# Two hybrid blocks on one core: repeated key heads projected once and copied inside SBUF, and the delta net's rates and products by beta placed elsewhere

## The reference, cut to what matters

```python
# first block, attention branches (of z = rms_norm(x) @ w_in)
q = partial_rope(q, cos, sin)                       # 4 heads of 64
k = partial_rope(k[:, :, None, :], cos, sin)[:, :, 0]     # ONE key head of 64 for the 4
iq = partial_rope(iq, icos, isin)                   # 8 index heads of 32
ik = partial_rope(ik[:, :, None, :], icos, isin)[:, :, 0] # ONE index key of 32 for the 8
sc = einsum('bqhs,bqh->bqs', relu(iq . ik * 32 ** -0.5), iw)   # the 128 largest are kept
out = softmax(q . k, kept) @ v * silu(g)
# second block
q = axial_rope(rmsnorm(aq, q_norm_w)); k = axial_rope(rmsnorm(ak, k_norm_w))
#   8 query heads, 2 key heads, 4 queries to a key
attn = softmax(q . k / 8) @ v
beta = sigmoid(b_raw); g = -exp(a_log) * softplus(a_raw + dt_bias)   # 2 directions x 8 heads
# delta net by chunks of 64 tokens, both directions:
L = where(strict, (k * beta) @ k.T * decay, 0); T = inverse(eye + L)
u = T @ (v * beta)
```

## Time and profile before

| | us |
|---|---|
| median of 3 runs | 2613.02 (2611.95 to 2616.01) |
| the profiled execution | 2617.88 |
| its span, first to last instruction | 2616.1 |
| TensorE busy | 2328.5 (89%) |
| VectorE busy | 989.2 (38%) |
| ScalarE busy | 453.4 (17%) |
| GpSimd busy | 218.0 (8%) |

### The profile page before, as it was taken

One profiled execution on the slowest core, in us unless ns is written; L12 is line 12 of the kernel. 1 busy time (PEld: TensorE's weight loads), 2 busy tenths in 40 slices (PEclk: granted clock), 3 DMA queues, 4 the chain that ended last, 5 costly groups with the idle time before them and its releaser, 6 DMA issues. The chain is left out here.

```text
span 2616.1 us, 44161 instructions
## 1 busy us (share of the span) xinstructions
PE 2328.5 (89%) x18735; PEld 1240.4 (47%) x18735; DVE 989.2 (38%) x1789; ACT 453.4 (17%) x851; POOL 218.0 (8%) x174
## 2 busy tenths in 40 slices
PE   7989989969898898987898977889979969999998
PEld 3543438624363343953444433589634444444442
DVE  1166785232026667523224442464321151111112
ACT  1011432010102143201122332222110020000000
POOL 0111300000010220000003630400000000000000
PEclk9999999989898999998988998899989979999999
DMA  4134010020214301002101101100013439999997
GB/s 151 57 146 160 9 45 3 23 81 32 101 45 180 131 4 44 4 22 89 65 25 57 49 25 53 45 3 5 34 65 121 198 139 401 421 422 422 422 422 301
DMA packets 60439, 328.25 MB, mean 125 GB/s; under 512 B 6880, under 2 KB 9440, under 8 KB 31200
## 3 DMA queue, kind: packets, MB, share of 16 engines
q1 hardware_dynamic: 60256, 325.63, 31.9%
HBM read 320.88 MB, written 4.72 MB: 124 GB/s over the span
## 5 line engine op out<-in xcount | busy, mean ns | idle before, releaser
L420 PE MATMUL ps<-store,side_ring 128*128 128x512 f32 x832 | 420.0, 630 | 20.5 <-DMA side_ring<-in_w_rwkv 8.1
L420 PEld LDWEIGHTS ps<-store,side_ring 128*128 128x128 f32 x832 | 146.6, 196 | 188.9 <-issue 165.3
L2346 PE MATMUL ps<-expert_ring,xe 128*64 128x512 f32 x1024 | 224.8, 597 | 2.7 <-DVE back L2455 1.7
L333 PE MATMUL ps<-store,side_ring 128*128 128x512 f32 x384 | 169.9, 606 | 1.9 <-DVE store L299 1.9
L2346 PEld LDWEIGHTS ps<-expert_ring,xe 128*64 128x64 f32 x1024 | 73.3, 138 | 150.8 <-issue 148.7
L333 PEld LDWEIGHTS ps<-store,side_ring 128*128 128x128 f32 x384 | 74.6, 195 | 96.1 <-issue 93.8
L2374 PE MATMUL ps<-expert_ring,store 128*64 128x512 f32 x512 | 113.2, 600 | 1.4 <-DVE store L2431 1.4
L1437 PE MATMUL ps<-store,weight_ring 128*128 128x512 f32 x256 | 112.0, 593 | 1.9 <-DVE store L299 1.9
L2116 PE MATMUL ps<-store,expert_ring 128*128 128x512 f32 x224 | 99.1, 606 | 11.6 <-DMA expert_ring<-in_w_merge 11.6
L420 PE MATMUL ps<-store 128*128 128x512 f32 x160 | 78.9, 647 | 12.6 <-DMA store<-in_w_merge 12.1
L2403 ACT ACTIVATE store<-ps 128x1024 f32<-128x1024 f32 x16 | 16.4, 1024 | 419.2 <-PE ps L2346 419.2
(11 more groups left out here) (420 smaller groups left out, 3885.8 us busy)
## 6 DMA issues: line engine op xcount, KB each, us to landing
expert_ring<-in_w_expert SPq DMA_DIRECT2D x192, 1024.0 KB, 16.2
mixed<-in_w_ada SPq DMA_DIRECT2D x24, 1024.0 KB, 5.0
side_ring<-in_w_attn SPq DMA_DIRECT2D x34, 512.0 KB, 3.6
side_ring<-in_w_rwkv SPq DMA_DIRECT2D x20, 512.0 KB, 4.4
weight_ring<-in_ple_gate SPq DMA_DIRECT2D x16, 512.0 KB, 3.4
side_ring<-in_w_conv SPq DMA_DIRECT2D x12, 512.0 KB, 3.3
store<-in_w_merge SPq DMA_DIRECT2D x10, 512.0 KB, 3.6
expert_ring<-in_w_merge SPq DMA_DIRECT2D x3, 1536.0 KB, 6.2
```

The lines of the kernel that those rows point to most:

```text
L333: last = nc.tensor.matmul(ps[:, u, :], ring[:, u, k, :], src[:, k, :], start=(k == 0), stop=(k == kt - 1))
L420: ins = self.nc.tensor.matmul(self.ps[:, self.banks[j % banks], :], self.ring[:, j % self.slots, k, :], self.src[:, k, :], start=(k == 0), ...
L2346: last = nc.tensor.matmul(ps[w, 2 * ep + half, :], xe[:, ep, k, :], ring[:, unit % SLOTS, k2, S * half:S * half + S], start=(k == 0), stop ...
```

## The change

In the first block A_K becomes one tile of the key head (rows 0 to 63) and the index key twice (rows 64 to 127); A_IK is a place in `z` that is no longer projected. The A_K tile is turned first, in two halves with their own tables, and SP copies the turned index key to four quarters of A_IK and the key head to rows 64 to 127 of A_K. The first gate tile moves into `project`, and its SiLU to the head of `index_topk`; the side work there has 9 tiles instead of 10. In the second block the two key heads share one tile (the query heads are put in pairs p and p + 4), so `normed_heads` has five tiles; the rates are 32 more columns of its values, copied by ScalarE, and the `by_head` tile is gone. They lie token-major, and four matmuls bring them into place. The product of `low` with beta moves to GpSimd in the spread stage, and `bv` to ScalarE in the chunk stage. The diff, cut to its core:

```diff
-A_Q, A_K, A_DQ, A_DK, A_IQ, A_IK, A_G, A_DG, N_A = 0, 2, 3, 6, 9, 11, 12, 14, 17
+A_Q, A_K, A_DQ, A_DK, A_IQ, A_G, A_IK, N_A = 0, 2, 3, 6, 9, 11, 13, 16
...
-    SEMAPHORES = dict(rotated=0, scaled=0, rot_used=0, added=0)
+    SEMAPHORES = dict(rotated=0, scaled=0, rot_used=0, added=0, ik_copied=0, k_copied=0)
+    KEYS = ((slice(0, HD), "head"), (slice(HD, P), "index"))
...
+    def parts(self, j):
+        table = self.jobs[j][1]
+        return self.KEYS if table == "keys" else ((slice(0, P), table),)
+
+    def parts_until(self, j):
+        return sum(len(self.parts(i)) for i in range(j))
+
...
     def rotate(self, pe, upto):
         for j in range(self.issued, upto):
-            tile, table = self.jobs[j]
+            tile = self.jobs[j][0]
             if j < 4:
-                pe.wait_ge(self.kept[0][j], self.kept[1])
+                bank = tile % 4
+                pe.wait_ge(self.kept[0][bank], self.kept[1])
             else:
-                pe.wait_ge(self.s["rot_used"], j - 3)
-            self.nc.tensor.matmul(self.M.ps[:, j % 4, :], self.M.c(f"rot_{table}"), self.z[:, tile, :], start=True,
-                                  stop=True).then_inc(self.s["rotated"], 1)
+                pe.wait_ge(self.s["rot_used"], self.parts_until(j - 3))
+            for rows, name in self.parts(j):
+                last = self.nc.tensor.matmul(self.M.ps[rows, j % 4, :], self.M.c(f"rot_{name}")[rows, rows], self.z[rows, tile, :],
+                                             start=True, stop=True)
+            last.then_inc(self.s["rotated"], 1)
...
+            for n, (rows, table) in enumerate(self.parts(j)):
+                if j or n:
+                    pool.wait_ge(self.s["scaled"], self.parts_until(j) + n)
+                self.nc.gpsimd.tensor_tensor(self.z[rows, tile, :], self.z[rows, tile, :], self.M.table(f"cos_{table}")[rows],
+                                             ALU.mult).then_inc(self.s["scaled"], 1)
...
+            for rows, table in self.parts(j):
+                self.nc.vector.tensor_tensor(self.turned[rows, j % 2, :], self.M.ps[rows, j % 4, :],
+                                             self.M.table(f"sin_{table}")[rows], ALU.mult).then_inc(self.s["rot_used"], 1)
+            dve.wait_ge(self.s["rot_used"], self.parts_until(j + 1))
+            dve.wait_ge(self.s["scaled"], self.parts_until(j + 1))
...
+    def repeat_keys(self, sp):
+
+        z = self.z
+        sp.wait_ge(self.s["added"], 1)
+        for q in range(4):
+            sp.dma_start(z[32 * q:32 * q + 32, A_IK, :], z[HD:HD + 32, A_K, :]).then_inc(self.s["ik_copied"], 16)
+        sp.wait_ge(self.s["ik_copied"], 64)
+        sp.dma_start(z[HD:P, A_K, :], z[0:HD, A_K, :]).then_inc(self.s["k_copied"], 16)
+        sp.wait_ge(self.s["k_copied"], 16)
...
+                if turn:
+                    turn.repeat_keys(sp)
...
+                nc.scalar.activation(raw_gate, raw_gate, ACT.Silu).then_inc(s["gate_ready"], 1)
...
+                act.wait_ge(s["gate_ready"], 1)
...
-            kept = project(nc, M, w_attn, A_G, KT, h, 4, keep, ready, ring)
-            turn = Turning(nc, M, z, [(t, "head") for t in range(A_IQ)] + [(t, "index") for t in range(A_IQ, A_IK + 1)], kept,
+            kept = project(nc, M, w_attn, A_G + 1, KT, h, 4, keep, ready, ring)
+            turn = Turning(nc, M, z, [(A_K, "keys"), (A_Q, "head"), (A_Q + 1, "head")] + [(t, "head") for t in range(A_DQ, A_IQ)]
+                           + [(t, "index") for t in range(A_IQ, A_IQ + 2)], kept,
...
-        side = SideProjection(nc, M, [silu(j) for j in range(A_G, N_A)] + [mixed(j) for j in range(early)], KT, h, ring,
+        side = SideProjection(nc, M, [silu(j) for j in range(A_G + 1, N_A)] + [mixed(j) for j in range(early)], KT, h, ring,
...
+        ring, w = sb("weight_ring", [P, 3, KT, P]), sb("token_weights", [P, KT, P + 32])
...
                 for i in range(n):
                     project(i)
-                    if 1 <= i <= 4:
+                    if i >= 1:
                         add_up(i - 1)
-                add_up(4)
-                spread(0, 0)
-                spread(1, 1)
                 pe.wait_ge(s["v_landed"], 16)
                 values(0)
-                add_up(5)
-                pe.wait_ge(s["kept"], 6)
-                spread(2, 2)
+                add_up(4)
+                values(1)
+                spread(0, 0)
+                pe.wait_ge(s["kept"], 5)
+                spread(1, 1)
                 pe.wait_ge(s["normed"], 1)
-                spread(3, 0)
-                values(1)
+                spread(2, 0)
+                spread(3, 2)
                 pe.wait_ge(s["normed"], 2)
                 rotate(0, 1)
                 pe.wait_ge(s["normed"], 3)
-                rotate(1, 2)
+                rotate(1, 0)
+                values(2)
                 pe.wait_ge(s["normed"], 4)
-                rotate(2, 0)
-                values(2)
+                rotate(2, 2)
                 pe.wait_ge(s["rot_used"], 1)
                 rotate(3, 1)
                 pe.wait_ge(s["rot_used"], 2)
-                spread(4, 2)
+                spread(4, 0)
+                values(3)
                 pe.wait_ge(s["rot_used"], 3)
-                spread(5, 0)
-                values(3)
-                pe.wait_ge(s["rot_used"], 4)
-                rotate(4, 1)
-                pe.wait_ge(s["normed"], 5)
-                rotate(5, 2)
+                rotate(4, 2)
...
+                    nc.scalar.activation(rates[:, t, :], ps[:, 4 + t, P:P + 32], ACT.Copy).then_inc(s["v_kept"], 1)
...
                     keep(i)
+                keep_values(0)
                 root(0)
-                keep(5)
-                keep_values(0)
+                keep_values(1)
                 root(1)
-                for t in range(1, TT):
+                for t in range(2, TT):
                     keep_values(t)
...
-            kv = pair // 2
-                jobs.append(Pair(q=z[:, pair, here], k=z[:, 4 + kv, :], keys=S, bias=None,
-                                 v=[(tok[:, t, HD * kv:HD * kv + HD],) * 2 for t in range(TT)],
+                jobs.append(Pair(q=z[:, pair, here], k=z[:, 4, :], keys=S, bias=None,
+                                 v=[(tok[:, t, 0:HD], tok[:, t, HD:P]) for t in range(TT)],
-        by_head = (a["w_ba2"], lambda act, made: nc.scalar.activation(rates, made, ACT.Copy))
-        side = SideProjection(nc, M, [mixed(j) for j in range(12)] + [by_head], KT, h, sb("side_ring", [P, 4, KT, P]), 4, (6, 7))
...
-                    for c in range(NCH):
-                        for w in halves:
-                            last = nc.tensor.matmul(ps[w, 0, 16 * c:16 * c + 16], rates[w, c * CH:(c + 1) * CH],
-                                                    M.c("ident2")[w, 0:16], start=True, stop=True)
+                    by_chunk = ps[:, 0, 0:16 * NCH].rearrange("p (t c x) -> p t c x", c=2, x=16)
+                    for hp, w in enumerate(halves):
+                        for c in range(2):
+                            last = nc.tensor.matmul(by_chunk[w, :, c, :], M.c("ident")[:, c * CH:(c + 1) * CH],
+                                                    rates[:, :, 16 * hp:16 * hp + 16], start=True, stop=True)
...
-                    pool.wait_ge(s["masked"], 2 * NCH)
+                        pool.wait_ge(s["masked"], 2 * n + 2)
+                        nc.gpsimd.tensor_tensor(low[:, n], low[:, n], beta[:, n].unsqueeze(3).broadcast_to([P, 2, JP, CH]),
+                                                ALU.mult).then_inc(s["by_beta"], 1)
+                    pool.wait_ge(s["by_beta"], NCH)
...
+                            pe.wait_ge(s["v_scaled"], 2 * JP * (c - 1))
...
+                @block.scalar
+                def _(act):
+                    for c in range(NCH):
+                        act.wait_ge(s["made"], c + 1)
+                        for d, n in ((0, c), (1, NCH - 1 - c)):
+                            for j in range(JP):
+                                nc.scalar.activation(bv[:, n, d, j, :], bank4(4 * (c % 2) + 3)[:, j, :], ACT.Identity,
+                                                     scale=beta[:, n, d, j:j + 1]).then_inc(s["v_scaled"], 1)
...
-                            own.mark(nc.vector.tensor_tensor(low[:, n, d], bank4(b), low[:, n, d], ALU.mult))
+                            own.mark(nc.vector.scalar_tensor_tensor(out=low[:, n, d], in0=bank4(b), scalar=-1.0, in1=low[:, n, d],
+                                                                    op0=ALU.mult, op1=ALU.mult))
                             own.mark(nc.vector.tensor_tensor(at[:, n, d], bank4(b + 1), at[:, n, d], ALU.mult))
                             own.mark(nc.vector.tensor_tensor(kd[:, n, d], bank4(b + 2), wide(decay_out), ALU.mult))
-                            own.step(nc.vector.tensor_tensor(bv[:, n, d], bank4(b + 3), wide(beta), ALU.mult))
```

(13 more changed lines are left out.)

55 lines of the change are left out of this document (22 added, 33 removed).

## The result

The changed kernel takes 2569.18 us (median of 4 runs, 2565.97 to 2569.99) against 2614.52 for the kernel before (2611.95 to 2617.49): a ratio of 0.9823, 95% interval 0.9808 to 0.9839. The forecast was 2570.2. The profiled execution has a span of 2567.9 us, 48.2 us under the one of before.

What follows compares the result with a forecast made beforehand. A chain of stages with barriers, each bound by its last engine: 14.9 + 8.0 + 7.6 + 13.3 - 0.2 - 0.8 = 42.8 us, from the median 2613.02 to 2570.2 us; range 2565 to 2582.

Steps and rivals of the forecast that it cites:

- Index stage and rotations: First block: TensorE ends the index stage, 6.8 us gained; halved rotations in the token stage save 0.6; 7.4 a layer.
- The two copies in series: Token stage: SP's key copies inside SBUF take some 5 us, hidden under 28 us of the same stage.
- Normed heads: Second block: five projected tiles for six, with two token products under the first inversion's wait; gain 8.0 us (6.5 to 8.5).
- Attention of the second block: Rate tile leaves the side work, 96 products for 104; the stage gains 7.6 us (4.6 to 8.8).
- about 1.5 us remain and 3 are gained: Second block's attention: of TensorE's 4.7 us of waits for ScalarE to free a bank, 3 us go (bounds 0 and 4.7).
- GpSimd is late next: End of the second block's attention: GpSimd ends last at 1543.8, VectorE at 1542.4 with one more 0.8 us step.
- Rival B: Second block's attention tail: bank waits stay, or GpSimd's last nine operations stretch; 3 to 4 us lost, 2574; chance 0.13.
- Chunk stage: Delta net's chunk products: TensorE replaces VectorE as bound, 2.42 us a chunk for 4.06; gain 13.3 us (9 to 14).
- Rival A: Chunk stage stays with ScalarE (2.75 us a chunk) or a half clock; 2.5 to 3.5 us come back, 2573; chance 0.17.
- Rates and spread: Rates stage: fewer matmuls gain nothing, side products wait for a load. Spread stage: beta on GpSimd costs 0 to 0.5, taken 0.2.
- Semaphores: Ends of stages: clearing costs 0.1 us per semaphore; eight more clearings lose 0.8 us.
- a sign of being wrong by over 5 us: Stages not touched: if one shifts its clock, the forecast is wrong by more than 5 us.

Runs made afterwards that it cites:

- e4: Changed kernel with a tenth side tile in the index stage of each layer: 2582.9 us, ratio 0.9869.
- e9: Changed kernel with the first two token products of the normed heads moved behind the second spread: 2569.48 us, ratio 0.9822.
- e2: Changed kernel with the two bv multiplications of a chunk back on VectorE: 2569.73 us, ratio 0.9819; chunk stage 27.91 us against 24.65.
- after's second: The changed kernel, unchanged, profiled once more: 2558.76 us in a single run, rates stage 29.89 us.
- after: The changed kernel itself, with the whole change, against the kernel before: 2569.18 us, ratio 0.9823.
- before again: The kernel before, unchanged, profiled once more: 2615.7 us in a single run; first block's attention 85.60 and 82.46 us.
- e1: Kernel before with only the delta net's part of the change: 2601.65 us, ratio 0.9945.
- e3: Changed kernel with the inputs' sizes of before as nearly as can be, no instruction different: 2568.28 us, ratio 0.981.

## Why the prediction was right, step by step

**Index stage and rotations.** As worked out, and confirmed by e4 and by the rotation group's 2.13 us. The two copies in series took 6.9 us and not 5, under the same cover. The SiLU ahead of the relus took 0.61 us, and ScalarE's idle time before the second pack went from 6.16 to 5.86: hidden.

**Normed heads.** 8.75 for 8.0, a quarter microsecond beyond the range given. The schedule held: counted from the fifth tile's end, the first spread came after 6.6 us (forecast 6.6), the end of four scalings after 11.2 (11.2), of the second inversion after 15.1 (15.3), of four turns after 21.4 (21.6), of the last add after 25.4 (25.9). The two products under the first wait do what it said, and e9 shows that it said too little: it left out the clock.

**Attention of the second block.** Near the number, by two errors that cancel. The step "about 1.5 us remain and 3 are gained" was wrong: 0.3 us remain, 4.4 are gained, and TensorE ends 12.5 us sooner in the stage (140.0 us in, 152.5 before), not 9.8 (6.8 and 4.4 make 11.2; of the other 1.3 us, part goes with the higher clock of the stage's first 10 us and the rest is open). The step "GpSimd is late next" was wrong as well: the tail behind TensorE's last product grew from 5.0 to 9.2 us because VectorE is last, 2.1 us behind GpSimd. The forecast gave VectorE one more step of 0.8 us behind the products; it has two more behind its last copy, and they take 6.45 us from first to last (1506.83 to 1513.28) where four took 3.10. They are also slower where GpSimd works beside them: the last four take 4.03 us, GpSimd being busy until 1511.15, and before, with GpSimd done at 1543.0, 3.10. Rival B named this tail with the wrong engine; its other half, that the waits for banks stay, fell with 4.7 going to 0.3.

**Chunk stage.** Right in size and mechanism. ScalarE needs 1.75 us a chunk (0.22 for each activation, 0.25 taken), TensorE 2.44 (2.42 taken), and it has no wait behind its first product. Rival A's half clock did not come: the stage begins at 0.50 in both kernels (2.4 us), and from 1652 on the granted clock is 1.00, where before it was 0.78 from 1686.3 to 1700.

The Trainium skill's page "ScalarE: Activation LUTs" ("What ACT_TABLE_LOAD costs") has figures from which the prediction estimated 0.24 us with one pointer; the trace has 0.22 (eight in 1.75 us). Its "Rules for kernel authors" would keep the multiplication on VectorE. Here, with ScalarE idle, e2 shows that this costs 3.3 us of the stage; the prediction had priced it at 5.

**Rates and spread.** GpSimd's multiplications by beta took 1.04 us each and the stage 0.5 more, the upper end of the term. The zero for the rates stage was wrong in this profile by 3.3 us (by 0.6 in after's second). It took the load's wait as given: the sixteen small matmuls' 1.1 us did go, but the wait went from 1.89 to 4.38 us, so the first product starts 1.35 us later in the stage, and the 32 records that took 15.84 us take 17.03, the first of them at half clock:

```profile
1564.64 17.03 PE L420 MATMUL ps<-store 128*128 128x512 f32 x32 [4.38 <-DMA store<-in_w_merge]
```

The rest is in the sums behind them (4.16 us for 3.63). In three profiles of kernels with the old arrays (before, before again, e1) its first product starts 3.53 to 3.59 us into the stage, and the stage takes 29.26 to 29.30; in after and its variants 3.59 to 5.36 us and 28.83 to 33.01. Whether the change makes that landing later on the whole can't be settled from these; e3 excludes nothing but the sizes of the arrays. Likewise 85.6 in the first block's attention came up three times in six with the old kernel's code, and never in the sixteen such stages of after and the variants that leave its loads alone.

**Semaphores.** The step failed. "0.1 us each" set the gap after a stage with 4 against one with 16. At the end of the token stage there are two more now, and the gap is 2.73 us (151.11 to 153.84) where it was 2.72; in the index stage one more, 2.15 against 2.14. The gap differs from stage to stage for another reason, and the 0.8 us were not there. In the chunk stage a fifth semaphore came to the four, and the gap went from 0.93 to 0.98. So the term of 0.8 us measures nothing that the runs show beyond that 0.05.

**What the sum left out.** It took every stage that isn't touched as constant, and named a shift of the clock in one of them as a sign of being wrong by over 5 us. That sign came. The two shifts, -5.6 and +3.3, and the 4.4 us by which after's second profile is shorter at the end of the program, are as large as the errors of all its terms. From profile to profile the gain is 48.2 us where 42.8 were forecast; between the medians it is 45.3. The total agreed within 1 us because the forecast started from 2613.02, the median of three runs, and a fourth run moved that median to 2614.52. On the median of four the sum is 2.5 us short, and the closer agreement is luck. The range's upper gain also left out the 15.5 us that the text allowed the first block (its sum took 14.9), which the rounding to 2565 covers.

## What to carry to other kernels

Price a removed product by the stage's last engine, and check what that engine was waiting for beside the product: in the second block's attention, bank waits of 4.4 us went with a tile of 6.8, and the tail on VectorE took 4.1 back. A transfer that is issued at a stage's start and needed by its first large product deserves a place in the stage before: here that was worth 3.1 to 3.8 us in each attention stage and 4 (against after's second profile) in the rates stage, with no arithmetic changed. Judge a change of a few microseconds by its own stage in the trace; repeats of one program differ by more than that elsewhere.

## What the runs showed of the hardware that was not expected

- With a load that lands 0.5 us later the stage is 3.1 us longer: TensorE, after waiting for it, stays at the lower of its two levels (1.2 GHz, granted clock 0.50) 3.5 us longer, and the stage takes one of a few lengths (79.3, 82.4 to 83.1, 85.6) and nothing between. With a wait of 4.24 us e4's layer 0 still took 82.41, and there the clock rose 7.9 us into the stage; in before's layer 0 it rose after 9.7 us, with a wait of 4.12, and the stage took 85.59; in after's layer 0 after 9.9 us, with a wait of 3.26, and it took 83.12. So neither the wait nor the clock decides alone.
- A small operation of VectorE's can take as long as the GpSimd operation that it begins beside: L673 took 1.28 us so, and 0.22 and 0.28 where it began 0.2 us before GpSimd's end (915.06 and 911.06 in before again). In before's layer 1 a delay of 1.1 us grew to 3.2 over three softmax jobs in which it did; the cause is read from the rows, not tested.
- A copy inside SBUF of 64 KB lands in 2.0 to 2.6 us and one of 128 KB in 2.3, beside matmuls, at no cost to them that the trace shows: 32 records of token products take 6.66 us beside the copies and took 6.66 before.
- ScalarE needs eight activations, 1.75 us, for what VectorE does in two operations issued 0.33 us apart. It was worth 3.3 us of the stage all the same, since the two engines ran side by side.
